# A four-layer transformer kernel: row factor of two norms applied after the gate and up products, and row factors by log and exp over 512 columns

## The reference, cut to what matters

```python
# layers 0 and 1
x = x + mixer(rms_norm(x, norm_mix[i]))
x = x + conv_ffn(rms_norm(x, norm_ffn[i]))
...
x = rms_norm(x, norm_final)
# layers 2 and 3
h = layer_norm(ALPHA * h + mixer(h), ln1_g, ln1_b)
h = layer_norm(ALPHA * h + conv_ffn_2(h), ln2_g, ln2_b)

rms_norm(x, g)      = x * rsqrt(mean(x*x) + 1e-6) * g
layer_norm(x, g, b) = (x - mu) * rsqrt(mean((x - mu)**2) + 1e-5) * g + b
conv_ffn(h)         = (silu(conv3(h @ w_gate)) * (h @ w_up)) @ w_down
```

## Time and profile before

| | |
|---|---|
| runs, us | 2650.45, 2652.37, 2658.81 (median 2652.37) |
| profiled execution, us | 2659.84 |
| its span, us | 2658.0 |
| PE busy, us | 2546.5 |
| POOL busy, us | 1793.7 |
| DVE busy, us | 1258.6 |
| ACT busy, us | 793.2 |

### The profile page before, as it was taken

How to read it: one execution, slowest core, us unless ns; L and a number is a source line. 1 busy time by engine, 2 the same in 40 slices (tenths; PEclk the granted TensorE clock), 3 DMA queues, 4 the chain that set the end, 5 groups by cost and what they waited for, 6 DMA issues and landing times.

```text
span 2658.0 us, 34453 instructions
## 1 busy us (share of the span) xinstructions
PE 2546.5 (96%) x12236; PEld 2130.7 (80%) x12236; DVE 1258.6 (47%) x1926; ACT 793.2 (30%) x1686; POOL 1793.7 (67%) x1581
## 2 busy tenths in 40 slices
PE   7789989999999899999999989999999999999998
PEld 5688878888887788888888767888887888788886
DVE  7967755333117743332078865333115445533312
ACT  2247652111006821110046642111005554211101
POOL 7756667666667777666678867666666567666662
PEclk9899999999999999999999999999999999999998
DMA  3210002222221022223221212222221112222222
GB/s 135 84 56 17 17 32 87 95 97 100 95 87 56 33 80 95 96 100 101 95 72 64 72 40 72 95 95 95 97 93 57 64 64 72 73 101 96 95 95 72
DMA packets 58119, 208.65 MB, mean 78 GB/s; under 512 B 6496, under 2 KB 6752, under 8 KB 58016
## 3 DMA queue, kind: packets, MB, share of 16 engines
q1 hardware_dynamic: 57744, 206.88, 22.9%
q10 hardware_dynamic: 272, 0.39, 0.0%
HBM read 205.09 MB, written 2.16 MB: 78 GB/s over the span
## 4 chain that ended last, share of the span: by engine, by line
PE 76%; DVE 12%; POOL 7%; ACT 3%; issue 2%; DMA 1%; SPq 0%; ACTq 0%; DVEq 0%; POOLq 0%
PE PS L803 22%; PE PS L804 22%; PE PS L805 22%; POOL WL L560 3%; DVE BLK L2157 2%; POOL WH L558 1%; PE PS L983 1%; PE PS L836 1%; DVE GTL L2264 1%; DVE NM L2207 1%; DVE RD L2504 1%; PE PS L1182 1%; DMA raw<-stream 1%; DVE PC L2450 1%; ACT GP L1558 1%
## 5 line engine op out<-in xcount | busy, mean ns | idle before, releaser
L560 POOL TENSOR_TENSOR WL<-raw,WH 128x1024 fp32r<-128x1024 f32 x380 | 918.9, 2418 | 31.7
L803 PE MATMUL PS<-HH,WH 128*128 128x512 f32 x2272 | 901.3, 397 | 31.7 <-POOL WL L560 8.7
L805 PE MATMUL PS<-HH,WL 128*128 128x512 f32 x2272 | 891.2, 392 | 0.0
L804 PE MATMUL PS<-HL,WH 128*128 128x512 f32 x2272 | 891.0, 392 | 0.0
L803 PEld LDWEIGHTS PS<-HH,WH 128*128 128x128 f32 x2272 | 430.8, 190 | 135.6 <-issue 18.7
L805 PEld LDWEIGHTS PS<-HH,WL 128*128 128x128 f32 x2272 | 430.2, 189 | 91.5
L804 PEld LDWEIGHTS PS<-HL,WH 128*128 128x128 f32 x2272 | 430.8, 190 | 85.6
L557 POOL TENSOR_TENSOR WH<-raw,SC 128x32 fp32r<-128x32 f32 x380 | 116.6, 307 | 506.6 <-DMA raw<-stream 488.6
L558 POOL TENSOR_SCALAR WH<-raw 128x992 fp32r<-128x992 f32 x380 | 409.2, 1077 | 0.0
L803 PE MATMUL PS<-GH,WH 128*128 (+1 forms) x704 | 273.9, 389 | 0.0
L804 PE MATMUL PS<-GL,WH 128*128 (+1 forms) x704 | 273.9, 389 | 0.0
(11 more groups left out here) (354 smaller groups left out, 3602.6 us busy)
## 6 DMA issues: line engine op xcount, KB each, us to landing
raw<-stream SPq DMA_DIRECT2D x380, 512.0 KB, 3.2
X<-x SPq DMA_DIRECT2D x4, 512.0 KB, 5.0
out<-X SPq DMA_DIRECT2D x8, 256.0 KB, 2.0
PR<-params SPq DMA_DIRECT2D x1, 536.0 KB, 7.1
spare_raw_nsa<-stream SPq DMA_DIRECT2D x1, 512.0 KB, 3.1
spare_raw_swa<-stream SPq DMA_DIRECT2D x1, 512.0 KB, 4.5
spare_raw_diff<-stream SPq DMA_DIRECT2D x1, 512.0 KB, 4.9
spare_raw_fox<-stream SPq DMA_DIRECT2D x1, 512.0 KB, 4.0
```

The costliest lines, as they stand in the source:

```text
L560: pool.tensor_tensor(WL[:, w], raw[:, w], hi.bitcast(F32), ALU.subtract).then_inc(chunk_split, 1)
L803: pe.matmul(to, h, his[k], start=start and k == 0, stop=False)
L804: pe.matmul(to, h, los[k], start=False, stop=False)
L805: last = pe.matmul(to, l, his[k], start=False, stop=stop and k == n_k - 1)
```

## The change

Two things. (a) In norms 1 and 3 (`LATE`), HH and HL are made from X times gain only, without the row factor, and can therefore be made before the sum of squares is known; the feed-forward multiplies each gate and up bank by the row factor (kept in SBUF as RB) in place. ACT writes X times gain twice, once as HH and once in fp32 to a PSUM bank, from which DVE takes the low part. The last output tile in layers 0 and 1 signals each of its eight k steps (`h_free`), since HH is overwritten behind it. The sums are made between the first four and last four k steps of the first gate and up pair. (b) In all norms the sums are made with the ones as weights, so that they come out over all partitions x 512 columns; the factor is exp(-0.5 * ln(mean + eps)), over 128x512 on ACT. The diagonals, their matmul, the reciprocal and the keep-busy matmuls ahead of the sums and before the factor are gone; those behind the sums stay in norms 2 and 4 to 7. Layer norms make mean squared and the negative mean on ACT over 512 columns, the variance on DVE in two instructions of 512 columns, and POOL centres tiles 5 to 7.

Cut to its core (declarations of semaphores, and asserts left out):

```diff
+LATE = (1, 3)
+LATE_AHEAD = 4
+
+
+def whole_norms(k):
+
+    return k - sum(x < k for x in LATE)
+
+
+CENTRED_BY_DVE = 5
...
+            def centre_late(k):
+
+                if NORMS[k][0] == "ln":
+                    pool.wait_ge(mean_kept, k - 4)
+                    for t in range(CENTRED_BY_DVE, KT):
+                        pool.tensor_tensor(tile(X, t), tile(X, t), WK[:, 4], ALU.add).then_inc(centred_pool, 1)
+
             def norm_lo(k):
 
+                centre_late(k)
                 for t in range(1, KT, 2):
                     pool.wait_ge(h_hi, KT * k + t + 1)
                     pool.tensor_tensor(tile(HL, t), normalised(k, t), tile(HH, t).bitcast(F32), ALU.subtract
...
+            centre_late(8)
...
             def norm(k):
 
                 ln = NORMS[k][0] == "ln"
-                if k:
-                    pe.wait_ge(x_updated, KT * (k - 1) + 4)
-                    keep_busy(7, 12)
                 if ln:
                     pe.wait_ge(x_added, (KT - 2) * (k - 4))
                     pe.matmul(PS[:, 2], ONE_F[:], WK[:, 5], start=True, stop=False)
                 pe.wait_ge(added, (KT - 2) * (k + 1))
-                for b in range(QT):
-                    pe.matmul(PS[:, 4 + b, 0:1], WK[:, 4, b * P:(b + 1) * P], ONE_F[:, 0:1], start=True, stop=False)
+                pe.matmul(PS[:, 4], ONE_F[:], WK[:, 4], start=True, stop=False)
                 if ln:
                     pe.wait_ge(x_updated, KT * k)
-                    for b in range(QT):
-                        pe.matmul(PS[:, 1, b:b + 1], WK[:, 5, b * P:(b + 1) * P], ONE_F[:, 0:1], start=True, stop=False)
-                        last = pe.matmul(PS[:, 1, b:b + 1], tile(X, KT - 1, b * P, P), ONE_F[:, 0:1], start=False, stop=True)
-                    last.then_inc(x_summed, 1)
+                    pe.matmul(PS[:, 2], ONE_F[:], tile(X, KT - 1), start=False, stop=True).then_inc(means_ready, 1)
                 pe.wait_ge(squared, KT * (k + 1))
-                for b in range(QT):
-                    last = pe.matmul(PS[:, 4 + b, 0:1], WK[:, 1, b * P:(b + 1) * P], ONE_F[:, 0:1], start=False, stop=True)
-                last.then_inc(summed, 1)
-                if ln:
-                    pe.matmul(PS[:, 2], ONE_F[:], tile(X, KT - 1), start=False, stop=True).then_inc(means_ready, 1)
-                if k:
-                    keep_busy(0, 4 if ln else 6)
-                pe.wait_ge(diag_ready, k + 1)
-                pe.matmul(PS[:, 3], ONE_F[:], WK[:, 5], start=True, stop=True).then_inc(scale_ready, 1)
+                pe.matmul(PS[:, 4], ONE_F[:], WK[:, 1], start=False, stop=True).then_inc(summed, 1)
                 if 0 < k < 8:
                     keep_busy(0, 18 if ln else 12)
+
+            def late_sums(k):
+
+                pe.wait_ge(squared, KT * (k + 1))
+                pe.wait_ge(added, (KT - 2) * (k + 1))
+                pe.matmul(PS[:, 4], ONE_F[:], WK[:, 4], start=True, stop=False)
+                pe.matmul(PS[:, 4], ONE_F[:], WK[:, 1], start=False, stop=True).then_inc(summed, 1)
...
-                    if t >= 6:
+                    if t >= 6 and q["kind"] in MERGED:
                         pe.wait_ge(x_updated, 2 * KT * n + t - 3)
                     pe.wait_ge(chunk_split, c + t + 1)
-                    products((c + t) % SLOTS, PS[:, out_bank(q["kind"], t)], h_his, h_los).then_inc(chunk_used, 1)
+                    if t == OUT_TILES - 1 and q["kind"] in GROUPED:
+                        for k in range(KT):
+                            last = products((c + t) % SLOTS, PS[:, out_bank(q["kind"], t)], [h_his[k]], [h_los[k]], 1,
+                                            k == 0, k == KT - 1, k)
+                            last.then_inc(chunk_used if k == KT - 1 else h_free, 1)
+                    else:
+                        products((c + t) % SLOTS, PS[:, out_bank(q["kind"], t)], h_his, h_los).then_inc(chunk_used, 1)
...
+                if late:
+                    pe.wait_ge(x_updated, 2 * KT * n + 4)
+                if late:
+                    first_two(c, h_wait(2 * n + 1), k1=4)
+                    late_sums(2 * n + 1)
+                    first_two(c, h_wait(2 * n + 1), k0=4)
+                else:
+                    first_two(c, h_wait(2 * n + 1))
...
-                norm(kn + 1)
+                if kn + 1 not in LATE:
+                    norm(kn + 1)
...
+            def late_hi(k, t):
+
+                if t < KT - 1:
+                    act.wait_ge(h_free, (KT - 1) * LATE.index(k) + t + 1)
+                else:
+                    act.wait_ge(chunk_used, layers[k // 2]["gu_chunk"])
+                act.activation(tile(HH, t), tile(X, t), ACT.Copy, scale=param("norms", NORMS[k][1] * KT + t)).then_inc(h_hi, 1)
+                if t >= 2:
+                    act.wait_ge(h_lo[t % 2], KT // 2 * k + t // 2)
+                act.activation(PS[:, 2 + t % 2], tile(X, t), ACT.Copy, scale=param("norms", NORMS[k][1] * KT + t)
+                               ).then_inc(staged, 1)
+
             def norm(k):
                 kind, gain, bias = NORMS[k]
-                act.preload_act_table(ACT.Sqrt)
+                act.preload_act_table(ACT.Ln)
                 for t in range(KT):
+                    if k in LATE and t == KT - 1:
+                        for h in range(LATE_AHEAD):
+                            late_hi(k, h)
                     if k == 0:
                         act.wait_ge(x_landed[t // 2], 16)
                     else:
                         act.wait_ge(x_updated, KT * (k - 1) + t + 1)
                     if t >= 2:
                         act.wait_ge(added, (KT - 2) * k + max(t - 2, 1))
-                    act.activation(WK[:, t % 2], tile(X, t), ACT.Square).then_inc(squared, 1)
+                    act.activation(WK[:, t % 2], tile(X, t), ACT.Square, scale=D ** -0.5).then_inc(squared, 1)
+                if k in LATE:
+                    for h in range(LATE_AHEAD, KT):
+                        late_hi(k, h)
                 if kind == "ln":
+                    act.wait_ge(means_ready, k - 4)
+                    act.wait_ge(added, (KT - 2) * (k + 1))
+                    act.activation(WK[:, 0], PS[:, 2], ACT.Square, scale=1.0 / D).then_inc(mean_squared, 1)
+                    act.activation(WK[:, 4], PS[:, 2], ACT.Copy, scale=-1.0 / D).then_inc(mean_kept, 1)
                     act.wait_ge(variances, k - 4)
-                    act.activation(ST[:, 0], ST[:, 3], ACT.Sqrt, bias=SC[:, SC_EPS + 1:SC_EPS + 2]).then_inc(rooted, 1)
+                    act.activation(WK[:, 5], WK[:, 5], ACT.Ln, bias=SC[:, SC_EPS + 1:SC_EPS + 2]).then_inc(logged, 1)
                 else:
                     act.wait_ge(summed, k + 1)
-                    act.activation(ST[:, 0], PS[:, 4:8, 0], ACT.Sqrt, bias=SC[:, SC_EPS:SC_EPS + 1], scale=1.0 / D
-                                   ).then_inc(rooted, 1)
+                    act.activation(WK[:, 5], PS[:, 4], ACT.Ln, bias=SC[:, SC_EPS:SC_EPS + 1]).then_inc(logged, 1)
+                act.wait_ge(logged, k + 1)
+                act.activation(RB[:] if k in LATE else PS[:, 3], WK[:, 5], ACT.Exp, scale=-0.5).then_inc(scale_ready, 1)
+                if k in LATE:
+                    return
...
-                    act.wait_ge(scaled_x, KT * k + t + 1)
+                    act.wait_ge(scaled_x, KT * whole_norms(k) + t + 1)
...
-                        act.wait_ge(chunk_used, i * 4 + (c + 2 * y + 1))
+                        if 2 * n + 1 in LATE:
+                            act.wait_ge(rescaled, i * 4 + (2 * n * FT + 2 * y + 1))
+                        else:
+                            act.wait_ge(chunk_used, i * 4 + (c + 2 * y + 1))
...
                 if kind == "ln":
-                    dve.wait_ge(x_summed, k - 4)
-                    own.link(dve.tensor_scalar(ST[:, 2], PS[:, 1, 0:QT], 1.0 / D, None, ALU.mult))
-                    own.link(dve.tensor_tensor(ST[:, 4], ST[:, 2], ST[:, 2], ALU.mult))
+                    dve.wait_ge(mean_squared, k - 4)
                     dve.wait_ge(summed, k + 1)
-                    own.link(dve.scalar_tensor_tensor(out=ST[:, 3], in0=PS[:, 4:8, 0], scalar=1.0 / D, in1=ST[:, 4],
-                                                      op0=ALU.mult, op1=ALU.subtract))
-                    dve.tensor_scalar(ST[:, 3], ST[:, 3], 0.0, None, ALU.max).then_inc(variances, 1)
-                    dve.wait_ge(means_ready, k - 4)
-                dve.wait_ge(rooted, k + 1)
-                own.link(dve.reciprocal(ST[:, 1], ST[:, 0]))
-                diagonals(WK[:, 5], ST[:, 1]).then_inc(diag_ready, 1)
+                    own.link(dve.scalar_tensor_tensor(out=WK[:, 5], in0=WK[:, 0], scalar=-1.0, in1=PS[:, 4],
+                                                      op0=ALU.mult, op1=ALU.add))
+                    dve.tensor_scalar(WK[:, 5], WK[:, 5], 0.0, None, ALU.max).then_inc(variances, 1)
+                if k in LATE:
+                    dve.wait_ge(scale_ready, k + 1)
+                    return
```

(33 more changed lines are left out.)

10 lines of the change are left out of this document (3 added, 7 removed).

## The result

The changed kernel takes 2634.48 us (median of 5 runs, 2630.13 to 2637.33), the kernel before 2650.60 (median of 5, 2647.08 to 2658.81): a ratio of 0.9930, 95% interval [0.9916, 0.9944], some 16 to 19 us less. Repeated on another occasion it was 0.9922 [0.9907, 0.9938]. The forecast was 2627 (2613 to 2643). Its sum was made for the profiled execution: 2634.8 forecast, 2636.23 found (span 2634.4), against 2659.84.

A forecast was written before the change was run, and what follows sets the result against it. The prediction took the number of matmuls on PE, plus what stands between products across each norm, to bound the kernel. Gains of 15.2 + 2.4 + 0 + 1.8 + 5.6 = 25.0 us from the median 2652.4 gave 2627.4, range 2613 to 2643.

The forecast's parts named there:

- Norms 1 and 3: Late factor takes the chain from sum to factor off PE's path: gains 7.0 and 8.2, together 15.2 us.
- The rival: ACT cannot run ahead at norms 1 and 3, so tiles come late: price 5 us, 2632.4; chance 0.10.
- The feed-forwards: Two more DVE instructions per pair cost nothing: 6.8 us of work against the 10.9 PE spends on a pair.
- Table load: A table load between log and exp at the norms, adding 1.3 us.
- the rival of a shared table: Log and exp share the loaded table; six norms save 1.3 us more each, 7.8: 2619.6; chance 0.17.
- Norms 2 and 4: Log and exp shorten the chain by 2.2 us each, less the clock's loss: 2.4 us gain together.
- the clock's price: At norms 2 and 4, low clock after the pause without keep-busy matmuls: 1.0 us each, between 0 and 4.4.
- Norms 5 to 7: Last X tile to first scaling gets shorter, 8.4 us in sum, less 2.4 for the clamp and 4.2 for the clock: 1.8.
- Norm 8: In the tail, first scaling comes 4.3 us earlier and the last result gains 1.3 more: 5.6 us together.
- Sum: All norms together: 15.2 + 2.4 + 0 + 1.8 + 5.6 = 25.0 us gained.
- The clock rival: Norms 2 and 4 to 7 lose 4.4 us each to the clock, 22 in place of 6.2: 2643.2; chance 0.11.

The follow-up runs named there:

- e1: The changed kernel with only the late factor at norms 1 and 3, other norms as in the kernel before: 2641.98 us, ratio 0.9949.
- e11: The changed kernel with ScalarE squaring the last tile at norms 1 and 3 before making any parts, not running four tiles ahead: 2642.86 us, ratio 0.9954.
- e8: The changed kernel with each rescale in the feed-forwards of layers 0 and 1 done three times: 2633.66 us, ratio 0.9922.
- e10: The changed kernel with each rescale in the feed-forwards of layers 0 and 1 done four times: 2639.73 us, ratio 0.9944.
- e3: The changed kernel with the table set holding both log and exp named outright: 2626.26 us, ratio 0.9890 to the kernel before.
- e4: The changed kernel with more keep-busy matmuls behind the sums, 24 for 12 at norms 2 and 4, 45 for 18 at 5 to 7: 2625.99 us.
- e7: The changed kernel with one log/exp table set, more keep-busy matmuls, and no variance clamp in norms 5 to 8: 2612.66 us, ratio 0.9843.

## Why the prediction was right, point by point

- **Norms 1 and 3: 15.2 forecast, 15.0 found** (7.0 and 8.0), alone (e1) and with the rest; 13.8 against the second profile of the kernel before. ACT ran ahead as worked out: tile 0 from 412.5, the late square at 417.4, the last low part made by 423.7, before PE asked. e11 shows that this was the condition: without it 11.4 us of the 15 are gone by starts, 8.5 by time. The rival was priced at 5: it had the wait too low (7.3) and left out the clock behind it (4.1).
- **The feed-forwards: no cost, found no cost** (233.69 us for the same products in both kernels). The forecast's sum of 6.8 us was made with the low part of the gated product at its short time of 0.69; the row was 8.8, since the earlier trace rows's stall does apply to L2673 (2.67). The room was there anyway: four more instructions per pair cost nothing (e8), six cost 0.1 to 0.2 us per pair (e10). The right term for the stall is not a price per instruction but the time at which POOL's instruction ends.
- **Table load: right.** Nine loads at the exp, 1.28 each; the rival of a shared table is out. The Trainium skill (ScalarE: Activation LUTs, the section on table sets) is right that one set serves both functions; e3 shows that it was not picked until it was named.
- **Norms 2 and 4: gaps 2.2 shorter, as forecast; the clock's price was the mis-sized term,** 1.0 each forecast, 2.8 and 1.6 found. So 2.4 forecast, 0.0 found. (At norm 2 the prediction read the gap as 9.9, from the X tile; by the last product at 786.44 it is 10.1. The sum does not use it.)
- **Norms 5 to 7: 1.8 forecast, 0.0 found.** Gaps got shorter by 1.5, 1.6 and 1.9, forecast 2.7, 1.7 and 1.6. At norm 5 the way from the last X tile to the first scaling took 7.2 us, clamp of 1.33 included, forecast 6.8 plus 0.5; what is missing is the last X tile, which came 1.2 us late against the kernel before. The first pairs lost 1.7, 1.8 and 1.6, forecast 1.4. The Trainium skill (TensorE: Matmul & The Clock Gate, what is actually happening) has the low clock as the state that activity must release, by which I put up to 2 us on each pause. Over five pauses that is 10 against the 6.2 charged, 3.8 less and not the 2.7 of the prediction; 9.5 were found, so it was nearer than my own term. e4 confirms the cause: activity in the pause gave 9 us back.
- **Norm 8: 5.6 forecast, 4.8 found** (3.6 against the second profile of the kernel before). The first scaling comes 7.3 us behind the last X tile (forecast 6.8, the clamp took 1.06 in place of 0.6); e7 gave 1.1 back. The prediction had no POOL beside it; but the change itself puts POOL's centring (L608) there, beside the clamp.
- **Sum.** 25.0 forecast, 19.7 found in the norms. The profiled execution came within 1.4 us of the forecast only because 3.9 us went elsewhere: that is luck. By medians 16.1 of the 25.0 came, and 2634.48 lies 7.1 above the 2627.4 forecast, inside the range. The late factor was right; of the log and exp part 9.8 was forecast and 4.7 found, nearly all behind norm 8. The halves add up: 13.1 (e1) and 7.6 (e2) by starts alone, 19.7 together.
- **The clock rival** (2643) had the right mechanism at half its price: the five norms lost 9.5 us of first pair, forecast 6.2, rival 22. At the same place and the same code the loss varied: norm 4 of the changed kernel took 12.8 us for its first pair, in e8 and e11 11.2.

## What to carry to other kernels

When a chain on which PE waits is made shorter, count what PE does in it before and after: filler that goes away with the chain can turn a shorter wait into a slower start, and busy time does not show it; products per microsecond and the granted clock do. Taking the factor off the path altogether was worth 14 to 15 us and had no such price, provided that the operands could be made ahead. Then look at what falls on what: an instruction that comes 1.3 us earlier can land in another engine's use of SBUF and give half of it back.
